# A state-space block's gate product and its 16 time-step columns, regrouped into three chunks and one of them moved ahead

## What is computed

```python
proj = x @ w_in
z, xbc, dt_raw = proj[..., :o1], proj[..., o1:o2], proj[..., o2:o3]
sc_b, sc_c, sc_h = proj[..., o3:o4], proj[..., o4:o5], proj[..., o5:]
...
xbc = silu(causal_dwconv(xbc, conv_w) + conv_b)
xs, bm, cm = ...
dt = softplus(dt_raw + dt_bias)
da = dt * -exp(a_log)
xdt = xs * dt[..., None]
a_cs = cumsum(da)
cb = einsum(cm, bm)
y_diag = einsum(cb * decay, xdt)
chunk_states = einsum(bm, xdt * decay_to_end)
y_off = einsum(cm, h_in) * exp(a_cs)
y = y_diag + y_off + xs * d_skip
y = y * silu(z)
```

## Time and profile before

| | |
|---|---|
| median of 3 runs | 1398.26 us (1396.3 to 1402.96) |
| profiled execution | 1399.13 us, its span 1397.3 us |
| PE busy | 1308.3 us (94%), 8203 matmuls |
| POOL, ACT, DVE busy | 952.9 (68%), 650.4 (47%), 423.2 us (30%) |
| chain that ended last | PE 83%, DVE 10%, ACT 4% of the span |
| POOL's splits (line 529) | 412 instructions, 952.6 us |
| ACT's roundings (line 544) | 412 instructions, 413.1 us |

### The profile page before, as it was taken

The page is one execution under the profiler, slowest core; times in us unless marked ns, Lnnn a source line. Parts: engine busy times, 40 slices in busy tenths (PEclk is TensorE's granted clock), DMA queues, the critical chain, the costliest instruction groups (busy, mean ns, idle before and its releaser), DMA issues.

```text
span 1397.3 us, 19619 instructions
## 1 busy us (share of the span) xinstructions
PE 1308.3 (94%) x8203; PEld 1164.4 (83%) x8203; DVE 423.2 (30%) x764; ACT 650.4 (47%) x836; POOL 952.9 (68%) x416
## 2 busy tenths in 40 slices
PE   7999997869899999999999999999989878999997
PEld 7888876647789998889799879999878757999885
DVE  3426125433523220016444250011032545011114
ACT  5663335544446554342544344444344654443533
POOL 6773426524787889874758867877966545886983
PEclk9999998979999999999999999999999999999999
DMA  8653215403555656553446575655647434664661
GB/s 267 188 152 105 84 54 150 134 30 121 158 181 153 195 181 203 188 166 116 136 113 192 196 237 147 191 155 175 224 137 223 150 91 113 186 172 140 213 203 46
DMA packets 118108, 218.86 MB, mean 157 GB/s; under 512 B 9433, under 2 KB 18948, under 8 KB 117892
## 3 DMA queue, kind: packets, MB, share of 16 engines
q1 hardware_dynamic: 113888, 209.94, 49.3%
q10 hardware_dynamic: 4132, 7.67, 1.7%
HBM read 216.53 MB, written 1.05 MB: 156 GB/s over the span
## 4 chain that ended last, share of the span: by engine, by line
PE 83%; DVE 10%; ACT 4%; issue 2%; DMA 1%; ACTq 0%; POOL 0%; SPq 0%; DVEq 0%
PE acc L1846 12%; PE acc L1848 12%; PE acc L1849 12%; PE acc L1839 10%; PE acc L1840 10%; PE acc L1841 10%; PE pm L1854 8%; PE acc L1797 2%; PE acc L1798 2%; PE acc L1799 2%; ACT pm L544 1%; PE pm L1763 1%; ACT whi L544 1%; DVE XTlo L1040 0%; PE pm L1871 0%
## 5 line engine op out<-in xcount | busy, mean ns | idle before, releaser
L529 POOL TENSOR_TENSOR wlo<-raw,whi 128x1024 fp32r<-128x1024 f32 (+2 forms) x412 | 952.6, 2336 | 429.9 <-ACT whi L544 428.3
L544 ACT ACTIVATE whi<-raw 128x1024 fp32r<-128x1024 f32 (+2 forms) x412 | 413.1, 1020 | 380.4 <-PE acc L1849 165.4
L1846 PE MATMUL acc<-XThi,whi 128*128 128x256 f32 x1424 | 407.4, 286 | 6.1 <-DVE XTlo L1023 3.2
L1848 PE MATMUL acc<-XTlo,whi 128*128 128x256 f32 x1424 | 405.9, 285 | 0.0
L1849 PE MATMUL acc<-XThi,wlo 128*128 128x256 f32 x1424 | 405.7, 285 | 0.0
L1846 PEld LDWEIGHTS acc<-XThi,whi 128*128 128x128 f32 x1424 | 276.3, 194 | 7.5 <-issue 3.7
L1848 PEld LDWEIGHTS acc<-XTlo,whi 128*128 128x128 f32 x1424 | 276.4, 194 | 0.2
L1849 PEld LDWEIGHTS acc<-XThi,wlo 128*128 128x128 f32 x1424 | 276.3, 194 | 0.0
L1839 PE MATMUL acc<-whi,XThi 128*128 128x512 f32 (+3 forms) x336 | 132.6, 395 | 2.9 <-POOL wlo L529 2.2
L1840 PE MATMUL acc<-wlo,XThi 128*128 128x512 f32 (+3 forms) x336 | 128.2, 381 | 0.0
L1841 PE MATMUL acc<-whi,XTlo 128*128 128x512 f32 (+3 forms) x336 | 127.9, 381 | 0.0
(11 more groups left out here) (405 smaller groups left out, 1655.9 us busy)
## 6 DMA issues: line engine op xcount, KB each, us to landing
raw<-in_w_in SPq DMA_DIRECT2D x68, 512.0 KB, 3.8
raw<-in_w_ff SPq DMA_DIRECT2D x64, 512.0 KB, 3.6
raw<-in_w_in_mix SPq DMA_DIRECT2D x44, 512.0 KB, 3.6
raw<-in_w_down SPq DMA_DIRECT2D x44, 512.0 KB, 4.3
raw<-in_w_gate SPq DMA_DIRECT2D x40, 512.0 KB, 3.7
raw<-in_w_up SPq DMA_DIRECT2D x40, 512.0 KB, 3.7
raw<-in_w_branch SPq DMA_DIRECT2D x16, 512.0 KB, 3.6
raw<-in_w_out_mix SPq DMA_DIRECT2D x16, 512.0 KB, 3.5
```

Source lines behind the costliest of these rows:

```text
L529: nc.gpsimd.tensor_tensor(wlo[:, u % SPLIT, 0:nk, 0:width], raw[:, u % RAW, 0:nk, 0:width], whi[:, u % SPLIT, 0:nk, 0:width].bitcast(F32), ...
L544: return nc.scalar.activation(out_, in_, func, **k)
L1846: T.matmul(o, wh[:, fs], hi[:, k, :], start=opens and f % 2 == 0, stop=False, skip_group_check=True)
L1848: T.matmul(o, wh[:, fs], lo[:, k, :], start=False, stop=False, skip_group_check=True)
```

## The change

The 1040 columns of z and dt_raw, before one chunk of 16 and two of 512, become three chunks. The first, still called "dt", has the 16 dt columns and the first 336 columns of z (two loads for each unit, through `pieces`); "mz0" and "mz1" have 344 columns of z each. "dt" moves ahead of "xbc2", between the second and third convolution chunk. PE's hand-written order follows: "dt", one unit of "xbc2", the 16 transposes, three units of "xbc2", "mz0", one unit of "mz1", the cb group, two units of "mz1", the states, the last unit of "mz1", the offsets, rows 0 and 1, one unit of "sc0", rows 2, and the head loop with the other three units of "sc0". DVE does the softplus ahead of the third convolution. ACT takes the silu of z in three parts: the first behind the softplus (`dt_done`), the second behind the third `silu2`, the third in the head loop. The outputs are the same.

```diff
+ZA, ZB = 336, 344
...
+    if width == SSD_H + ZA:
+        return (c0, SSD_H), (0, ZA)
...
     for c in range(3):
+        if c == 2:
+            g.append(("dt", "w_in_mix", KD, M_DT, SSD_H + ZA, "T"))
         g.append((f"xbc{c}", "w_in_mix", KD, M_XBC + c * W, W, "F"))
-    g.append(("dt", "w_in_mix", KD, M_DT, SSD_H, "T"))
     for c in range(2):
-        g.append((f"mz{c}", "w_in_mix", KD, c * W, W, "T"))
+        g.append((f"mz{c}", "w_in_mix", KD, ZA + c * ZB, ZB, "T"))
...
+            silu2(0)
+            turn("p0", PThi)
+            high_halves(landed("xbc1") + AHEAD)
+            silu2(1)
+            high_halves(landed("dt") + AHEAD)
             logs()
             fn(ea2[:], headv("ssd_a_log"), ACT.Exp)
             act.wait_ge(S["dt_in"], 1)
             fn(sp_y[:], sp_y[:], ACT.Exp, scale=-1.0).then_inc(S["dt_e"], 1)
-            high_halves(begun("mz0", 2) + AHEAD)
+            high_halves(begun("xbc2", 2) + AHEAD)
+            act.wait_ge(S["dt_done"], 1)
+            fn(zz[:, :, 0:ZA], accT("dt")[:, :, SSD_H:], ACT.Silu).then_inc(evac_at("dt")[0], 1)
+            high_halves(landed("xbc2") + AHEAD)
+            silu2(2)
+            leave("mz0", zz[:, :, ZA:ZA + ZB], ACT.Silu)
+            logs()
+            high_halves(begun("mz1", 1) + AHEAD)
             act.wait_ge(S["s_bt"], 1)
             fn(bmt[:], pm[:, 1, 0:2 * P], ACT.Copy).then_inc(S["s_btc"], 1)
             act.wait_ge(S["s_acc"], 1)
             fn(eac[:], acs[:, 1:3, :], ACT.Exp).then_inc(S["s_eac"], 1)
-            high_halves(begun("mz1", 1) + AHEAD)
+            high_halves(begun("mz1", 3) + AHEAD)
...
                 if hb == 1:
-                    leave("mz0", zz[:, :, 0:W], ACT.Silu)
-                    leave("mz1", zz[:, :, W:D], ACT.Silu)
+                    leave("mz1", zz[:, :, ZA + ZB:D], ACT.Silu)
...
             product("xbc1", XThi, XTlo)
             pe.wait_ge(S["p_in"], 16)
             turn("p0", pin)
-            product("xbc2", XThi, XTlo, 0, 3)
+            product("dt", XThi, XTlo)
+            product("xbc2", XThi, XTlo, 0, 1)
...
             last.then_inc(S["s_xs"], 1)
-            product("xbc2", XThi, XTlo, 3, 4)
-            product("dt", XThi, XTlo)
-            from_x("mz0", 0, 2)
+            product("xbc2", XThi, XTlo, 1, 4)
+            from_x("mz0")
+            from_x("mz1", 0, 1)
             pe.wait_ge(S["s_xd"], 2)
...
-            from_x("mz0", 2, 4)
-
+            from_x("mz1", 1, 3)
             pe.wait_ge(S["s_btc"], 1)
             pe.wait_ge(S["s_xe"], 1)
...
-            from_x("mz1", 0, 1)
+            from_x("mz1", 3, 4)
             pe.wait_ge(S["s_stc"], 1)
...
-            from_x("mz1", 1, 2)
             rows(0)
             rows(1)
-            from_x("mz1", 2, 4)
+            from_x("sc0", 0, 1)
             rows(2)
             for hb in range(8):
                 if hb in (0, 3, 6):
-                    from_x("sc0", hb // 3, hb // 3 + 1)
+                    from_x("sc0", hb // 3 + 1, hb // 3 + 2)
```

More of the change, by code:

```diff
@@ L65, in pieces @@
 def pieces(c0, width):
-    return ((c0, ABC), (O_FF, DN_H)) if width == ABC + DN_H else ((c0, width),)
+    if width == ABC + DN_H:
+        return (c0, ABC), (O_FF, DN_H)
+    if width == SSD_H + ZA:
+        return (c0, SSD_H), (0, ZA)
+    return ((c0, width),)
 def gemm_plan():
@@ L435, in build @@
             a_o a_hi a_lo f_sq f_ss f_rn f_xn f_t f_tc f_cum f_d s_sq s_ss s_rn s_v s_w s_wt s_mx s_m s_hi s_lo
-            g_done f1_r f1_hi f1_lo silu2 p_in dt_in dt_e dt_g s_cb s_xs s_xsc s_xd s_bt s_btc s_ac
+            g_done f1_r f1_hi f1_lo silu2 p_in dt_in dt_e dt_done s_cb s_xs s_xsc s_xd s_bt s_btc s_ac
             s_acc s_eac s_xe s_st s_stc s_yo s_yod b_row b_e0 b_e b_m b_y b_yd y_z y_ss y_n c_out c_hi c_lo
@@ L1476, in _ @@
                     turn("p0", PThi, PTlo)
+                    v.wait_ge(S["w_used"], landed("dt"))
+                    gd = accT("dt")[:, :, 0:SSD_H]
+                    link(V.tensor_tensor(gd, gd, headv("ssd_dt_bias").unsqueeze(1).to_broadcast([P, NT, SSD_H]),
+                                         ALU.add))
+                    link(V.tensor_copy(logit[:], gd))
+                    V.scalar_tensor_tensor(out=sp_y[:], in0=gd, scalar=-1.0, in1=logit[:], op0=ALU.mult,
+                                           op1=ALU.max).then_inc(S["dt_in"], 1)
                     v.wait_ge(S["s_xs"], 1)
@@ L1481, in _ @@
                                         per_head(headv("ssd_d")), ALU.mult)
[L1482 to L1495, removed]
+                    v.wait_ge(S["dt_e"], 1)
+                    softplus = softplus_tail(logit[:], sp_y[:], SSD_H,
+                                             acc[:, chunks["dt"][0] % 2, 0, SSD_H + ZA:BANK], 0, 32)
+                    V.tensor_copy(dtv[:], softplus)
+                    V.scalar_tensor_tensor(out=da[:], in0=softplus, scalar=-1.0,
+                                           in1=ea2[:].unsqueeze(1).to_broadcast([P, NT, SSD_H]),
+                                           op0=ALU.mult, op1=ALU.mult).then_inc(S["dt_done"], 1)
+            v.wait_ge(S["dt_done"], 1)
             for t in range(NT):
@@ L1567, in finished @@
                 link(V.tensor_tensor(pm[:, 2, :], pm[:, 2, :], y, ALU.add))
-                v.wait_ge(*evac_at(f"mz{b % 2}"))
+                v.wait_ge(*evac_at("dt"))
+                for c in range(2):
+                    v.wait_ge(*evac_at(f"mz{c}"))
                 V.tensor_tensor(y, pm[:, 2, :], zz[:, b // 2, (b % 2) * W:(b % 2 + 1) * W], ALU.mult)\
@@ L2198, in _ @@
                     rows(hb + 3)
-            from_x("sc0", 3, 4)
             from_x("sh0")
```

## The result

| | before | changed |
|---|---|---|
| median | 1397.13 us (10 runs) | 1389.22 us (10 runs) |
| lowest, highest | 1394.54, 1403.37 | 1387.85, 1394.03 |
| ratio to before | | 0.9945 (95%: 0.9929 to 0.9961) |
| profiled execution, its span | 1399.13, 1397.3 | 1387.88, 1386.1 |
| PE, POOL busy in the span | 1308.35, 952.85 | 1300.9, 953.4 |

What follows compares the result with a forecast made beforehand. PE was taken to bound the kernel around the change. Old products 33.9 us, less 23.2 for the new, 0.8 for tails and 1.6 of new wait, gave 8.3 us gained: 1398.3 to 1390.0 us, range 1386.5 to 1396.

Steps and rivals of the forecast that it cites:

- Added, 23.2 us: PE's time for 48 matmuls of 352 columns and 96 of 344, priced on a line between neighbouring widths: 23.2 us.
- New wait, 1.6 us: PE ahead of the states waits for DVE's xe, which follows ACT's longer queue: 1.6 us, between 0.5 and 2.9.
- Covers: Other engines' chains that PE's new order should hide; four thin ones were claimed free by 0.4 to 1.4 us.
- rival 1: Thin covers fail and xe may meet a whole split: about 3 us lost, gain 5, 1393.3 us; chance 0.24.
- Free by 1.4 us: "dt" bank read out before "mz0": 7.2 us on DVE and ACT against 8.6 us of PE's "xbc2" units.
- Free by 0.4: x times dt before the cb group: DVE's 9.3 us from the end of "xbc2" against PE's 9.7 us.
- The bank of the second convolution: Ahead of "xbc2": DVE empties the bank at 649.59, PE arrives at 650.5; free by 0.9 us.
- the unit of "xbc2" behind the transposes: Split ready at about 654.1 after ACT's silu and POOL's work, PE wants it at 655.1; free by 1.0 us.
- rival 3: Clock falls elsewhere: PE at the 1.2 GHz level through the head loop, 19 us more, 1409 us; chance 0.04.
- rival 4: Gain does not reach the end, as a later stage is bound by something unmoved: 1397 us; chance 0.05.
- rival 2: More comes back: xe meets no split, matmuls cost by columns alone (0.155 us at 344); gain 10.1, 1388.2; chance 0.07.
- 16.43 us: Kernel before, PE's time in "dt" and two of eight z units, put down to narrow matmuls, half clock, late split.

Runs made afterwards that it cites:

- 400 first: Changed kernel with the first z part at 400 columns and the others at 312, instead of 336 and 344: stretch 73.69 us, median 1390.39 us, ratio 0.9947.
- wide "dt" alone: Kernel before with its dt chunk at 256 columns instead of 16, 240 of them not read: stretch 81.93 us, median 1398.71 us, ratio 1.0006.
- regrouped only: Kernel before with chunks of 352, 344 and 344 columns, dt at its old place, PE's order kept: stretch 79.32 us, median 1395.57 us, ratio 0.9987.
- moved only: Changed kernel with dt back at 16 columns at its new place and z as two chunks of 512: stretch 78.02 us, median 1393.74 us, ratio 0.9971.
- 208 first: Changed kernel with the first z part at 208 columns and the others at 408, instead of 336 and 344: stretch 73.48 us, median 1388.40 us, ratio 0.993.

## Why the prediction was right, and where it was not

- **The result.** 1389.2 us against 1390.0, in the range. In the stretch 7.66 us against 8.3.
- **Added, 23.2 us.** Measured 7.82 for the chunk with "dt" and 0.158 for each of 96 others, 23.0. The line between neighbours was right.
- **New wait, 1.6 us.** It came, at its place and by its mechanism, with 2.15 us, inside 0.5 to 2.9. Counted from the end of "xbc2", PE was to begin the states at 16.9 us and began at 17.47. The term that was mis-sized is `xe`: 2.31 us taken, 2.70 measured. It began 0.12 us later than worked out, and 0.15 us between its end and PE's start were left out; 0.1 had been added by rounding. These 0.57 us are most of the 0.64 that the gain fell short. The 0.2 us that the matmuls cost less gave nothing back: PE only came to this wait sooner.
- **Covers.** All four held, so rival 1 did not come about, but two by less than claimed. "Free by 1.4 us" for the "dt" bank was 0.3: the softplus was priced by its old place, where its 32-column operation met only the last 0.3 us of a split of POOL's (5.1 us measured for 4.1), and the D products by their length instead of their start (0.2 us). "Free by 0.4" for x times dt was 0.06. "400 first" shows what comes just past it: a wait of 0.3 us. The bank of the second convolution was free by 1.0 (0.9 forecast), and the unit of "xbc2" behind the transposes was split 1.0 us ahead of its use (1.0 forecast).
- **Clock.** 1.00 from 642 to 715, the head loop too; rival 3 did not come.
- **The head loop.** 2.5 us as left. The work from "sh0" on kept its length within 0.1 us, so rival 4 did not come; rival 2 did not either, since `xe` met a split and 344 columns cost 0.158 us and not 0.155.
- **The step that failed is the reading, not the sum.** The prediction put 16.43 us down to "dt" and two z units as PE's own cost: narrow matmuls, half clock, unsplit weights. Taking away the narrow matmuls at their old place gave nothing (wide "dt" alone, -1.25 us) or 1.36 us (regrouped only), because the cb group may not start before `xdt`, and that ends 16.2 us behind "xbc2" at the least (16.2 in the one, 16.8 in the other), with the late split close beside it. The prediction added up DVE's chain for the changed kernel (9.3 us) but never for the kernel before (6.9 for the convolution, 2.8 to the start of the softplus behind ACT's exponential, 4.1, and 2.35 for `xdt`, the same 16.2). Had it done so, it would have seen that each half is worth little alone. The sum came out right, and not by luck: it took the old stretch as measured and checked the new one against its chains. The change does both at once: it takes the softplus out of the chain (16.4 to 9.5 us from the end of "xbc2" to the cb group) and gives PE 9.5 us of full-speed work of the same length to cover it.
- **Parts.** Alone they give 1.36 + 2.66 = 4.0 us, together 7.66. The other 3.6 belong to neither: as I read the traces, moving opens the place and regrouping fills it without the half clock.

## What to carry to other kernels

When PE is busy all the time at a low clock, look whether it is slow or only filling: compare when it arrives at its next wait with when the other engines' chain ends, in the kernel before and not only in the changed one. If the two agree within a tenth of a microsecond, speeding up PE there gives idle time, and here the idle time cost clock as well (3.2 us in "regrouped only"). Look for a second chain that ends beside the first.

Narrow products can be carried as extra columns of a wide chunk (here worth 5.0 us once the chunk had moved, 1.4 us ahead of that), and an operation with a long chain behind it (softplus here) belongs where no one needs it soon. Before giving an in-order queue a gate that waits on another engine, see which short, urgent instruction stands behind it: here the exponential of 32 columns, for 2 us with the splits that went the same way.

## What the runs showed of the hardware

- **Price by width.** One matmul start to the next, with new weights each time, at the full clock: 0.11 us at 16 and at 224 columns, 0.12 at 256, 0.146 at 312, 0.158 at 344, 0.161 at 352, 0.185 at 408, 0.188 at 416 (400 first), 0.231 at 512. So none of these widths costs less than about 0.11, and from 256 columns on the price is nearly a straight line. The Trainium skill (TensorE: Matmul & The Clock Gate, Back-to-back issue gap) gives columns over 2.4 GHz plus about 2.5 ns at the full clock, and calls this the gap of an isolated matmul. No width here agrees with it: by that rule it would be 0.149 us at 352 columns, an estimate. The section says of a stream with weight loads that the rule counts too little at few columns and too much at 512 (about 131 ns there). The rows agree with the first and not with the second: 0.231 us at 512.
- **The clock falls in two ways.** It falls while PE issues 16-column matmuls without a gap, to the 1.2 GHz level: 0.50 in "moved only". At the same place 224 columns (208 first) keep 1.00, and 352 do; at the old place 256 do ("wide dt alone"). And it falls behind idleness: 0.58 and 0.63 in "regrouped only" after 5.2 us of waits in 7.32, 0.62 in "wide dt alone" after 3.1 us of waiting.
 The Trainium skill (TensorE: Matmul & The Clock Gate, What's actually happening) names idleness as what brings the lower clock. The second kind of fall agrees with that; the first had no idleness ahead of it.
- **DVE beside POOL.** `xe`, the same instruction with the same operands, both in SBUF, took 1.22 to 1.24 us in five kernels where it did not start during a split of POOL's or only in its last 0.15 us, and 2.31 us before, 2.70 in the changed kernel, 2.44 and 3.23 with 400 and 208 first and 3.37 in "wide dt alone". In each of the long cases it ended some 1.1 us behind the end of the split that was running, and POOL's next split then took 3.3 to 3.4 us instead of 2.4. The 32-column operation on `logit` took 0.36, 0.97, 1.37 and 2.07 us in four kernels, and ended each time within 0.1 us of the end of a split. The length of such an operation in one kernel is no price for it in another where the other engine's timing moves.
